# A two-layer decoder trunk on one core: high and low part of the activations in one 512-column product

## The reference, cut to what matters

```python
def hybrid_mixer(h, w_in, b_in, ...):
    z = h @ w_in + b_in                      # 1024 x 7936: a, q, k, v, the short convolution, three gates
    a = z[..., 0:512] * sigmoid(z[..., 512:1024])
    a = causal_depthwise_conv(a, a_conv_w) + a_conv_b          # 31 taps, 512 channels
    y_a = silu(layer_norm(a, a_ln_g, a_ln_b)) @ a_w_out
    ...                                      # y_b from the attention, y_c from the short convolution
    gates = sigmoid(z[..., OFF_G:].reshape(bsz, s, 3, 1024))
    return (gates[..., 0, :] * y_a + gates[..., 1, :] * y_b + gates[..., 2, :] * y_c) @ w_o

for layer in range(2):
    x = x + hybrid_mixer(rms_norm(x, ...), ...)
    x = x + memory_cross_attention(rms_norm(x, ...), rms_norm(mem, ...), wq, wk, wv, wo)
    x = x + (swiglu if layer == 0 else moe_swiglu)(rms_norm(x, ...), ...)
return rms_norm(x, final_g)
```

## Time and profile before

| | |
|---|---|
| median of 3 runs | 1944.98 us |
| the profiled execution | 1943.2 us |
| its span | 1941.1 us |
| TensorE busy | 1919.0 us, 99% |
| VectorE busy | 1491.5 us, 77% |
| ScalarE busy | 1203.8 us, 62% |
| DMA, mean over the span | 269 GB/s |
| mean granted clock of TensorE | 0.997 |

### The profile page before, as it was taken

The page is one execution under the profiler, slowest core; times in us unless marked ns, Lnnn a source line. Parts: engine busy times, 40 slices in busy tenths (PEclk is TensorE's granted clock), DMA queues, the critical chain, the costliest instruction groups (busy, mean ns, idle before and its releaser), DMA issues.

```text
span 1941.1 us, 29617 instructions
## 1 busy us (share of the span) xinstructions
PE 1919.0 (99%) x12070; PEld 1734.9 (89%) x12070; DVE 1491.5 (77%) x1310; ACT 1203.8 (62%) x1045; POOL 64.7 (3%) x79
## 2 busy tenths in 40 slices
PE   8999999999999999999999999999999999999998
PEld 8999999999999999999988888888888888888886
DVE  7977765464458977864578888888888888888886
ACT  6445645453445454754467777777777777777775
POOL 2000000000001000000000000001000000000000
PEclk9999999999999999999999999999999999999999
DMA  8443554345544444444489999999999999999992
GB/s 318 156 166 123 187 182 166 131 174 184 184 151 182 174 142 162 174 179 148 141 357 400 366 392 370 400 362 375 391 361 399 370 377 384 362 405 384 372 387 110
DMA packets 75407, 521.50 MB, mean 269 GB/s; under 512 B 9264, under 2 KB 9264, under 8 KB 14000
## 3 DMA queue, kind: packets, MB, share of 16 engines
q1 hardware_dynamic: 72320, 509.15, 68.7%
q0 software_dynamic: 2992, 11.01, 2.0%
HBM read 512.79 MB, written 7.34 MB: 268 GB/s over the span
## 4 chain that ended last, share of the span: by engine, by line
PE 93%; DVE 3%; ACT 2%; POOL 1%; issue 0%; DMA 0%; SPq 0%; ACTq 0%; DVEq 0%
PE bank L1487 29%; PE bank L1489 28%; PE bank L1488 28%; DVE wlo L915 2%; ACT whi L500 1%; PE bank L1904 1%; PE bank L1704 1%; PE bank L1684 1%; PE bank L1623 1%; PE bank L1598 1%; DMA raw<-in_stream 0%; POOL U L426 0%; PE bank L1563 0%; PE bank L1596 0%; DVE U L941 0%
## 5 line engine op out<-in xcount | busy, mean ns | idle before, releaser
L915 DVE TENSOR_TENSOR wlo<-raw,whi 128x2048 fp32r<-128x2048 f32 x479 | 1090.5, 2282 | 310.2 <-ACT whi L500 309.5
L500 ACT ACTIVATE whi<-raw 128x2048 fp32r<-128x2048 f32 x479 | 913.5, 1909 | 271.4 <-PE bank L1489 266.0
L1487 PE MATMUL bank<-whi,act_hl 128*128 128x512 f32 (+1 forms) x1472 | 568.4, 386 | 0.8
L1489 PE MATMUL bank<-whi,act_hl 128*128 128x512 f32 (+1 forms) x1472 | 560.9, 381 | 0.0
L1488 PE MATMUL bank<-wlo,act_hl 128*128 128x512 f32 (+1 forms) x1472 | 560.4, 381 | 0.0
L1487 PE MATMUL bank<-h_hl,whi 128*128 128x256 f32 x1472 | 419.5, 285 | 1.6 <-DVE wlo L915 1.3
L1488 PE MATMUL bank<-h_hl,whi 128*128 128x256 f32 x1472 | 416.5, 283 | 0.0
L1489 PE MATMUL bank<-h_hl,wlo 128*128 128x256 f32 x1472 | 416.5, 283 | 0.0
L1487 PEld LDWEIGHTS bank<-whi,act_hl 128*128 128x128 f32 x1472 | 277.5, 189 | 55.6 <-DVE wlo L915 4.1
L1489 PEld LDWEIGHTS bank<-whi,act_hl 128*128 128x128 f32 x1472 | 277.3, 188 | 53.7
L1488 PEld LDWEIGHTS bank<-wlo,act_hl 128*128 128x128 f32 x1472 | 277.6, 189 | 51.7 <-issue 0.7
(11 more groups left out here) (246 smaller groups left out, 1170.9 us busy)
## 6 DMA issues: line engine op xcount, KB each, us to landing
raw<-in_stream SPq DMA_DIRECT2D x475, 1024.0 KB, 6.6
raw<-in_stream SPq DMA_DIRECT2D x6, 512.0 KB, 3.7
U<-in_stream SPq DMA_DIRECT2D x2, 1024.0 KB, 11.2
xacc<-U POOLq DMA_DIRECT2D x3, 512.0 KB, 6.9
xT<-in_x_cols SPq DMA_DIRECT2D x2, 512.0 KB, 5.2
memhat<-in_mem_cols SPq DMA_DIRECT2D x1, 1024.0 KB, 20.3
hrow<-U POOLq DMA_DIRECT2D x1, 1024.0 KB, 5.7
memhat<-in_stream SPq DMA_DIRECT2D x1, 1024.0 KB, 9.0
```

The lines of the kernel that those rows point to most:

```text
L500: act.activation(whi[:, n % SPLIT, 0:words], src[:, 0:words], ACT.Copy).then_inc(hi_ready, 1)
L915: dve.tensor_tensor(wlo[:, n % SPLIT, 0:words], src[:, 0:words], whi[:, n % SPLIT, 0:words].bitcast(F32), ALU.subtract).then_inc(lo_ready, 1)
L1487: pe.matmul(o, st[0], mv[0], start=start, stop=False, **kw)
L1489: return pe.matmul(o, st[1], mv[0], start=False, stop=stop, **kw)
```

## The change

It has five parts.

1. For most dense chunks (`WIDE`, without ga 3, xk 0 and xo 3) the two products with the same stationary block `st[0]` become one product of 512 columns (`both`), with the high and the low part of the tokens as one moving operand. The third keeps 256 columns. Its sum lands in the first half of a bank, high times low in the second half, so each output block has a bank of its own and a chunk fills two banks. That holds for 37 chunks in each layer and for 20 of the 22 gate and up chunks of the dense SwiGLU.
2. The halves are added as they leave PSUM: ScalarE copies the first half into SBUF, with the bias where there is one, VectorE adds the second half to it. For wo and xo VectorE adds both halves to x, one after the other.
3. The sigmoid of the gates is a ScalarE instruction of its own, in SBUF, behind the split of the next chunk (`after_split`).
4. In the SwiGLU gate has banks 0 and 1, up has banks 2 and 3, in every block; TensorE waits for `gate_raw` and `up_raw`, which say that the block before has left them. The first block still has three products of 256 columns.
5. `CONV_A_AT` spreads the same 124 taps anew; two uses of PSUM banks behind the attention move to other banks.

```diff
-CONV_A_AT = dict(zip(range(3, 28), (6, 8, 8, 8, 8, 8, 8, 3, 4, 6, 3, 6, 8, 3, 0, 0, 3, 0, 0, 6, 3, 5, 8, 8, 4)))
+CONV_A_AT = dict(zip(range(3, 28), (6, 6, 6, 4, 6, 6, 6, 3, 4, 6, 4, 6, 9, 3, 0, 6, 5, 0, 5, 6, 3, 6, 6, 6, 6)))
...
+WIDE = ("q", "k", "cb", "cc", "ch", "gc", "gb", "ga", "xk", "wo", "xq", "xo")
+GATES = [what for what in PLAN if what[0] in ("gc", "gb", "ga") and what != ("ga", 3)]
...
+        def wide(n):
+
+            what = PLAN[local(n)[1]]
+            return what[0] in WIDE and what not in (("ga", 3), ("xk", 0), ("xo", 3))
+        def halves(n):
+
+            two = psum[:, 2 * (n % 2):2 * (n % 2) + 2, :]
+            return two[:, :, 0:256], two[:, :, 256:512]
+
+        def summed(n):
+
+            return wide(n) and kind(n) not in ("wo", "xo")
...
-            return kind(n) in ("aval", "ch", "v", "cout", "bout", "aout") or (unscaled(n) and kind(n) == "agate")
+            return wide(n) or kind(n) in ("agate", "aval", "v", "cout", "bout", "aout")
...
+                elif summed(n):
+                    if what == "ch":
+                        act.wait_ge(pads, 2 * (lay + 1))
                     if what == "ga":
                         act.wait_ge(gated, 8 * lay + i + 1)
-                    take(n, [gates[:, 2 * i + k, :] for k in range(2)], ACT.Sigmoid, lay, blk)
-                elif what in ("xk", "xq", "xv"):
-                    src = bank[2 * (n % 2)][:].rearrange("p (a b) -> p a b", a=2)
-                    dst = {"xk": kx[:, 2 * i:2 * i + 2, :], "xq": qx[:, 2 * i:2 * i + 2, :],
-                           "xv": vx[:, :, 256 * i:256 * i + 256]}[what]
-                    act.activation(dst, src, ACT.Copy).then_inc(out_act, 1)
+                    first, to = halves(n)[0], whole(lay, what, i)
+                    if what in ("xk", "xq"):
+                        act.activation(to, first, ACT.Copy).then_inc(half_s, 1)
+                    else:
+                        for k in range(2):
+                            ins = act.activation(to[:, k, :], first[:, k, :], ACT.Identity, bias=bias(lay, 2 * blk + k))
+                        ins.then_inc(half_s, 1)
...
+                if wide(n) and PLAN[c] in GATES:
+                    what, i = PLAN[c]
+                    s_, val = taken(n)
+                    act.wait_ge(s_, val)
+                    act.activation(whole(lay, what, i), whole(lay, what, i), ACT.Sigmoid).then_inc(sig, 1)
...
+            def ffn_half(to, at, used, done):
+
+                act.wait_ge(w_used, used)
+                act.activation(to.rearrange("p (a b) -> p a b", a=2), psum[:, at:at + 2, 0:256], ACT.Copy).then_inc(done, 1)
+
+            def ffn_act(i, j):
+
+                act.wait_ge(gate_raw, i + 1)
+                act.activation(sil[:, j, :], sil[:, j, :], ACT.Silu).then_inc(silu_s, 1)
...
             def residual(n, lay, pair):
                 xb = xT[:, 2 * pair:2 * pair + 2, :]
-                dve.tensor_tensor(xb, bank[2 * (n % 2)][:].rearrange("p (a b) -> p a b", a=2), xb, ALU.add)\
-                   .then_inc(x_ready, 1)
+                if wide(n):
+                    first, second = halves(n)
+                    mine(dve.tensor_tensor(xb, first, xb, ALU.add))
+                    settled()
+                    dve.tensor_tensor(xb, second, xb, ALU.add).then_inc(x_ready, 1)
+                else:
...
+                elif summed(n):
+                    to = whole(lay, what, i)
+                    dve.wait_ge(half_s, half_at(n))
+                    dve.tensor_tensor(to, halves(n)[1], to, ALU.add).then_inc(out_dve, 1)
...
+            def ffn_gate(i, j, used=None, first=False):
+
+                to = sil[:, j, :].rearrange("p (a b) -> p a b", a=2)
                 if first:
+                    dve.wait_ge(w_used, used)
+                    ins = dve.tensor_tensor(to, bank[1][:].rearrange("p (a b) -> p a b", a=2),
+                                            rstd[:].unsqueeze(1).to_broadcast([P, 2, S]), ALU.mult)
                 else:
+                    dve.wait_ge(gate_half, i)
+                    ins = dve.tensor_tensor(to, psum[:, 0:2, 256:512], to, ALU.add)
+                ins.then_inc(gate_raw, 1)
+
+            def ffn_dve(i, j, used=None, first=False):
+
+                to = gf[:, j, :].rearrange("p (a b) -> p a b", a=2)
+                if first:
+                    dve.wait_ge(w_used, used)
+                    ins = dve.tensor_tensor(to, bank[3][:].rearrange("p (a b) -> p a b", a=2),
+                                            rstd[:].unsqueeze(1).to_broadcast([P, 2, S]), ALU.mult)
+                else:
+                    dve.wait_ge(up_half, i)
+                    ins = dve.tensor_tensor(to, psum[:, 2:4, 256:512], to, ALU.add)
+                ins.then_inc(up_raw, 1)
+                dve.wait_ge(up_raw, i + 1)
+                dve.wait_ge(silu_s, i + 1)
+                dve.tensor_tensor(gf[:, j, :], gf[:, j, :], sil[:, j, :], ALU.mult).then_inc(g_s, 1)
...
+            def both(o, st, mv, start, stop):
+
+                pe.matmul(o[:].rearrange("p (a b) -> p a b", a=2), st[0], mv, start=start, stop=False)
+                return pe.matmul(o[:, 0:256], st[1], mv[:, 0, :], start=False, stop=stop)
...
+                        if wide(n):
+                            ins = both(bank[2 * (n % 2) + o], wt(n, k, 256, 128 * o, 128), h_hl[:, :, k, :],
+                                       k == 0, k == DB - 1)
...
+                    def up(n0, value, bk, evicted, count, first=False):
+
+                        pe.wait_ge(lo_ready, value)
+                        pe.wait_ge(evicted, count)
+                        for o in range(2):
+                            for k in range(DB):
+                                if first and o == 0 and k % 2 == 0:
+                                    pe.wait_ge(h_lo_s, 8 + k // 2 + 1)
+                                ins = both(bank[bk + o], wt(n0, k, 256, 128 * o, 128), h_hl[:, :, k, :], k == 0, k == DB - 1)
...
-                            up(f + 2 + c, 6 * i + f + 3 + c, bk + 1, parts_ready=(h_lo_s, 8) if first and j == 1 else None)
-                            up(f + 3 + c, 6 * i + f + 4 + c, bk)
+                            up(f + 2 + c, 6 * i + f + 3 + c, 0, gate_raw, 2 * i + j, first and j == 1)
+                            up(f + 3 + c, 6 * i + f + 4 + c, 2, up_raw, 2 * i + j)
```

161 lines of the change are left out of this document (81 added, 80 removed).

## The result

The changed kernel takes 1954.05 us (median of 5 runs, 1952.05 to 1955.38), the kernel before 1944.98 (5 runs on the same chip, 1943.79 to 1946.99). The ratio is 1.0045, with a 95% interval of 1.003 to 1.0059: slower by 9 us, where I had forecast 2.5 us faster. Both profiled executions are ordinary ones of their kernel: 1954.35 us with a span of 1952.5 for the changed one, 1943.2 and 1941.1 before.

What follows compares the result with a forecast made beforehand. The prediction took TensorE to bound the kernel: 19.0 us from longer products plus 0.5 at k 2, less 7.4, 5.9, 2.5 and 1.9 at four chains, saves 1.8. It forecast 1942.5 us, range 1930 to 1953.

Steps and rivals of the forecast that it cites:

- What bounds the kernel: Whole kernel: TensorE, busy 99% of the span; time is lost where it meets new waits; experts stay at 960 us.
- What a matmul costs: Wide chunks: two 256-column products becoming one of 512 save 0.0126 us, 0.20 us a chunk, 19.0 us over 94 chunks.
- The two-piece operand: 512-column product in wide chunks: bounds 0.2270 us (one contiguous product) and 0.2396 us (two products); the lower was taken.
- the third rival: Wide chunks: two-piece operand streams no faster than two products, starts 0.24 us apart; 14 us slower, 1958; chance 0.07.
- The chains: Four places where TensorE waits for the added work: 7.4, 5.9, 2.5 and 1.9 us given back.
- xq 0: From wo to xq 0, both layers: lagging residual and last addition give back 3.7 us, 7.4 in two layers.
- aout 0: From ga 1 to aout 0, both layers: low part of a comes late, 2.95 us idle TensorE per layer, 5.9 in all.
- the SwiGLU's first chunk: From xo to the SwiGLU, layer 0: additions of xo 0, 1 and 2 lengthen a binding round; 2.5 us given back.
- The second gate chunk: Layer 0's SwiGLU: it waits for eviction of the first gate chunk's banks; 1.9 us given back at most.
- The first rival: At the four chains: additions better hidden than walked; 1927.5 us, or 1934 at half the prices; chance 0.18.
- the second: In q, k and the gates: additions hold the banks, waits of 0.4 us a chunk; 8.6 slower, 1953; chance 0.13.
- the sum: Whole kernel: 19.0 + 0.5 - 7.4 - 5.9 - 2.5 - 1.9 = 1.8 us saved.

Runs made afterwards that it cites:

- e5_group16: Changed kernel with each chunk's sixteen 512-column products issued before its sixteen 256-column ones, in all wide chunks but xk and one interrupted by the square sum; 1950.89 us.
- e1_contig: Changed kernel with the high and low part of h side by side in memory, so the 512-column operand is one unbroken row; 1952.06 us.
- e4_narrow: Changed kernel with 24 of 94 wide chunks, those ahead of the three chains, back to three 256-column products and one copying engine; 1937.1 us.
- e9_ga: Changed kernel with only ga 0 and ga 1 (both layers, 4 chunks) back to three 256-column products and one copying engine; 1946.39 us.
- e12_taps: Changed kernel with the convolution's taps spread over the chunks as in the kernel before; 1958.53 us.
- e6_busy: Changed kernel with identity products, none longer than its wait, ahead of aout 0 and xq 0 and in the third step of layer 0's SwiGLU; 1952.66 us.
- e3_warm: Changed kernel with identity products meant to fill TensorE's waits at the three chains, but twice as long as the waits; 1976.18 us.
- e8_threes: Changed kernel with its copies, additions and waits, but each 512-column product issued as two of 256 columns into the same bank; 1960.24 us.

## Why the prediction was wrong, step by step

1. **What bounds the kernel.** Right: TensorE did, and time was lost only where it met new waits. The experts kept their 960 us, within 0.5.
2. **What a matmul costs: the step that failed first.** "Two products of 256 become one of 512: 0.0126 us" is true of rows of equal products, and e5_group16 shows 0.227 and 0.120 us with the very operand of this change. It is true of 14 of the 94 chunks in the changed kernel, and not of the other 80, whose alternating products take 0.353 us the pair. Each row I used was of a uniform stream, and I carried it over to a mixed one without a bound for the mixture. Forecast 19.0 us, measured 11.2. By the formula of the page "TensorE: Matmul & The Clock Gate" of the Trainium skill (Back-to-back issue gap) the matmuls saved would be worth an estimated 3.8 us; the trace lies between.
3. **The two-piece operand.** The lower bound I chose holds (e1_contig, e5_group16), so the third rival named nearly the right symptom, a distance of 0.236 in 80 of the 94 chunks, for a wrong reason.
4. **The chains.** Right in mechanism and size: xq 0 3.17 us late per layer for 3.7 given back, aout 0 2.67 for 2.95, the SwiGLU's first chunk 2.4 for 2.5. Sum 14.1 for 15.8, or 14.5 with the 0.4 that the four wide chunks directly ahead saved. That they are made by the additions ahead of them is shown by e4_narrow and, for aout 0, by e9_ga alone. The second gate chunk, 1.9, did not show in the changed kernel, and did show with 1.9 in e4_narrow, where nothing else hides it. The first rival (better hidden) and the second (banks held) did not come true; the second's point was nearly reached at k 2, where the old taps bring a wait of 2.9 us (e12_taps).
5. **What the sum left out.** Behind each wait I let TensorE go on at its old pace, at no cost and without a reason. It does not: 8.5 us of the 11.4 are the lower clock. The section The HAM clock gate of the same page of the Trainium skill says that an idle TensorE loses its clock and gets it back by working. The trace agrees: 1.00 ahead of the waits, 0.50 to 0.63 behind them, and 1.00 again a few us later. I read the waits of the kernel before, up to 1.5 us in that chunk, behind which the clock had stayed at 1.00, and did not ask what 2.6 to 3.5 us would do. That the pause is what costs the clock is shown by e6_busy for aout 0 of layer 0 and both xq 0 (5.7 of the 8.5 us); for the 2.7 us in the SwiGLU's first chunk it is argued from the likeness.
6. **The rest.** The opening of the kernel, 1.1 us later, before any wide chunk: over the twelve experiments the start of q 0 lies anywhere from 40.3 to 42.5 us (before 40.4, changed 41.5), with no relation to what was edited behind it, so most of this belongs to the single execution.

The sum had the span shrink by 1.8 us and it grew by 11.4, 13.2 apart: +7.8 from the wide chunks (19.0 less 11.2), +8.5 from the clock, +1.1 opening, -2.1 at the second gate chunk (nothing lost where 1.9 was forecast, and a later wait 0.2 shorter), -1.3 chains (14.5 for 15.8), -0.5 experts; that is 13.5. I had the chance of "slower" at 0.22, 0.20 of it from two mechanisms that did not happen. The range ended at 1953.0, a microsecond below the time.

## What to carry to other kernels

Price an instruction from a row in which it stands between the same neighbours as in the new kernel, and where there is none, give the mixture a bound of its own. Price a new wait of TensorE as long as those here (2.6 to 3.5 us) at up to twice its length (an estimate: 3.5 us cost 2.6 more at xq 0 of layer 1), since the stretch behind it may run at the lower clock, and look whether a few chunks left as they were take the wait away: here making 24 of the 94 chunks wide saved some 2.5 us and cost 19 in waits and clock (1954.05 - 1937.1 = 17, with the 2.5 on top). A cost that is hidden behind another loss, as the second gate chunk was, comes out when the other is mended.

## What the runs showed of the hardware

- 512-column and 256-column products in turn run at one of two paces, with the same instructions: 353.3 ns a pair (350, 361, 349) in 80 wide chunks of the changed kernel, 346.6 in 14; in e1_contig 70 and 24. In rows of sixteen (e5_group16) 0.227 (after about six) and 0.120, 0.347 together.
- A moving operand of 512 columns in two pieces of 256, 2048 elements apart, is as fast as an unbroken one: 0.227 us.
- Behind pauses of 2.6 to 3.5 us the granted clock mostly fell to the 1.2 GHz level for some us, at a cost of 1.5 to 2.6 us each; filled with small products the same pauses cost nothing behind them (e6_busy). A pause of 2.6 us did it in one run and not in another, one of 3.47 us in e3_warm did not, and the 2.4 us at aout 0 in e8_threes did not in either layer.
- The granted clock also fell without a pause, behind 32 products of ten columns in 4.6 us (kernel before, 986.8 to 993.6 us at 0.50).
- A 128x128 float32 product of the identity appears as two matmul records and takes 0.23 us (0.115 each) at full clock.
